# A hybrid decoder step on one core: one step boundary of the sample work removed on TensorE, two reductions moved on VectorE

## The reference

```
u = rms_norm(x);  proj = u @ w_in                        # 1024 -> 3592 columns
h_m = sigmoid(mo) * mlstm(mq, mk, mv, mi, mf, C, n, m)   # 4 heads of 64
h_r = retention(rope(rq), rope(rk), rv, S)               # 4 heads of 64
h_a = window_attention(aq, ak, av, k_buf, v_buf, ...)    # 8 heads, 2 kv heads, window 128
mix = concat(head_norm(h_m) * silu(mz), head_norm(h_r) * silu(rz), h_a * silu(az))
x   = x + mix @ w_out                                    # 1024 -> 1024
```

```
scores = einsum('bhtd,bhsd->bhts', qc, kc) * d_mat
o = einsum('bhts,bhse->bhte', scores, vc) + inter * einsum('bhtd,bhde->bhte', qc, S)
S_new = full * S + einsum('hs,bhsd,bhse->bhde', tail, kc, vc)
```

## Time and profile before

| what | value |
|---|---|
| runs of the kernel | 2145.33, 2147.58, 2148.93 us; median 2147.58 |
| the profiled execution, own time | 2145.33 us |
| its span, first to last instruction | 2143.5 us |
| PE busy | 2052.6 us (96%) |
| DVE busy | 1563.1 us (73%) |
| ACT busy | 881.6 us (41%) |
| POOL busy | 326.0 us (15%) |
| mean granted TensorE clock | 0.980 of full speed |
| output stage of layer 0 / layer 1, from their first matmuls | 872 / 1921 us |

### The profile page before, as it was taken

The page is one execution under the profiler, slowest core; times in us unless marked ns, Lnnn a source line. Parts: engine busy times, 40 slices in busy tenths (PEclk is TensorE's granted clock), DMA queues, the critical chain, the costliest instruction groups (busy, mean ns, idle before and its releaser), DMA issues.

```text
span 2143.5 us, 36369 instructions
## 1 busy us (share of the span) xinstructions
PE 2052.6 (96%) x12946; PEld 1159.4 (54%) x12946; DVE 1563.1 (73%) x3802; ACT 881.6 (41%) x2302; POOL 326.0 (15%) x352
## 2 busy tenths in 40 slices
PE   4799999999999999999988999999999999999997
PEld 2465555655555565444555555555565556554453
DVE  5777777777777777766365777777777777778866
ACT  5744444444444445331156444444444444461100
POOL 1111111111111111120010211111111111111200
PEclk9899999999999999999999999999999999999999
DMA  7411111111111114585541111111111111137642
GB/s 252 116 29 32 32 42 34 37 31 31 31 31 31 32 39 120 140 257 137 153 156 63 32 32 32 31 31 31 41 31 31 36 36 41 51 119 166 174 121 94
DMA packets 191788, 158.38 MB, mean 74 GB/s; under 512 B 151319, under 2 KB 165336, under 8 KB 191516
## 3 DMA queue, kind: packets, MB, share of 16 engines
q1 hardware_dynamic: 175684, 125.42, 21.7%
q0 software_dynamic: 7424, 29.43, 3.9%
q10 hardware_dynamic: 8568, 2.18, 0.5%
HBM read 85.35 MB, written 42.29 MB: 60 GB/s over the span
## 4 chain that ended last, share of the span: by engine, by line
PE 83%; DVE 12%; issue 2%; ACT 2%; DMA 1%; SPq 0%; DVEq 0%; ACTq 0%
PE J L544 51%; PE J L1257 12%; PE W L936 3%; PE W L956 3%; DVE W L537 2%; PE W L946 1%; PE W L1059 1%; PE W L1047 1%; PE W L1018 1%; PE J L993 1%; DVE ST L1805 1%; PE W L1038 1%; ACT junk L446 1%; DMA sc_xr<-in_x_sample 1%; PE W L922 1%
## 5 line engine op out<-in xcount | busy, mean ns | idle before, releaser
L544 PE MATMUL J<-W,x_mix 128*128 128x512 f16 (+2 forms) x3072 | 612.7, 357 | 5.9 <-ACT PB L1376 3.9
L544 PE MATMUL J<-W,uT_mix 128*128 128x512 f16 (+2 forms) x3072 | 613.5, 357 | 2.7 <-DVE W L537 2.6
L544 PEld LDWEIGHTS J<-W,x_mix 128*128 128x128 f16 x3072 | 300.0, 99 | 278.9 <-issue 14.9
L544 PEld LDWEIGHTS J<-W,uT_mix 128*128 128x128 f16 x3072 | 300.0, 99 | 276.3 <-issue 15.1
L1376 ACT ACTIVATE PB<-J,out_scale 128x512 f32<-128x512 f32 (+2 forms) x256 | 154.7, 604 | 357.6 <-PE J L544 348.9
L1257 PE MATMUL J<-W,EM_qkR_mix 128*128 128x512 f16 x480 | 115.6, 379 | 0.0
L1735 DVE TENSOR_TENSOR ge<-ge,gr 128x512 f32<-128x512 f32 (+1 forms) x96 | 57.4, 598 | 59.3 <-ACT gr L1313 59.3
L1346 ACT ACTIVATE ST<-ST,small 128x1024 f16<-128x1024 f32 x32 | 36.8, 1148 | 151.7 <-DVE small L1821 151.7
L1341 ACT ACTIVATE sc_xr<-sc_xr,small 128x128 f32<-128x128 f32 x256 | 98.6, 389 | 0.0
L1257 PE MATMUL J<-W,x_mix 128*128 128x512 f16 x400 | 97.9, 384 | 0.0
L1257 PE MATMUL J<-W,uT_mix 128*128 128x512 f16 x400 | 96.9, 381 | 0.0
(11 more groups left out here) (463 smaller groups left out, 3508.0 us busy)
## 6 DMA issues: line engine op xcount, KB each, us to landing
W<-in_w_in POOLq DMA_DIRECT2D x8, 2048.0 KB, 12.0
mix_d<-ST SPq DMA_DIRECT2D x32, 512.0 KB, 2.6
sc_xr<-in_x_prompt SPq DMA_DIRECT2D x20, 512.0 KB, 3.7
sc_xr<-x SPq DMA_DIRECT2D x20, 512.0 KB, 3.4
ST<-in_w_in POOLq DMA_DIRECT2D x4, 2048.0 KB, 12.9
W<-in_w_out SPq DMA_DIRECT2D x4, 2048.0 KB, 7.7
PB<-in_x_prompt SPq DMA_DIRECT2D x6, 512.0 KB, 3.7
x<-PB SPq DMA_DIRECT2D x6, 512.0 KB, 3.5
```

Of the source, the lines that this page charges most:

```text
L544: mm = nc.tensor.matmul(out, stationary(k, a), moving[:, k, b, :], start=(k == 0 and n == 0), stop=(k == KT - 1 and n == 2))
```

## The change

On PE the boundary between the sample's attention scores and the transposes of the rotated rows is removed: both are now in slot 9's step (before: slots 9 and 10). On DVE `inter(4)` and `inter(5)` leave slot 16's step, get a boundary of their own (`yield 13`) behind the mLSTM's state update, and so stand in slot 18's step. No arithmetic is changed.

```diff
@@ on_pe
                             kTS[64 * kv:64 * kv + 64, b, :], start=True, stop=True)
                 last_mm.then_inc(raised("scores_psum"), 1)
-                yield 5
-
                 pe.wait_ge(*seen("rope_done", layer))
                 for t in range(4):
                     last_mm = nc.tensor.transpose(T[1][:, 256 + t * TS:256 + (t + 1) * TS], PS[:, RQ + t * P:RQ + (t + 1) * P], idt)
@@ on_dve
                 V.tensor_tensor(sc, sc, bc(rden, WINDOW + DEC_SEQ), ALU.mult).then_inc(raised("pnorm"), 1)
-                inter(4)
-                inter(5)
                 yield 12
 
                 st(V.tensor_tensor(nu, nu, bc(tok[0:TS, 4:8], HD + 1), ALU.mult))
@@ on_dve
                 V.tensor_tensor(nst.rearrange("p k b -> p (k b)"), nst.rearrange("p k b -> p (k b)"),
                                 B[3][:, 260:276], ALU.add).then_inc(raised("state_m"), 1)
+                yield 13
+
+                inter(4)
+                inter(5)
                 yield 15
```

## The result

The changed kernel takes 2159.04 us (median of 5 runs, 2155.6 to 2160.3), the kernel before 2147.58 us (2145.33 to 2148.93). The ratio is 1.0054, 95% interval 1.0040 to 1.0069: slower by 11.5 us, where 9.6 were forecast. The profiled execution after has a span of 2155.5 us, 12.0 more than before. PE is busy 2058.6 us of it instead of 2052.6, with the same 12946 instructions.

The account below looks back on a forecast made before the run. PE, busy 96% of the span, was taken as the bound. Terms 2.5 + 1.5 + 0 + 4.1 + 1.5 = 9.6 us moved the median from 2147.58 to 2157.2 us, range 2152.5 to 2160.7.

Parts of the forecast that it names:

- Slot 9's wait: Layer 0: PE waits for POOL's rotation until about 937.8 instead of 935.31 for the maxima; slot 11 is 2.5 us late.
- The clock behind it: After PE stands about 4.9 us in layer 0's slot 9, the clock drops to 1.2 GHz and recovers; 1.5 us, bounds 0 and 3.0.
- Slot 10 in layer 1: Rotation long done and PE without idle; the same 0.39 us of transposes comes one slot earlier, costed at nothing.
- Layer 0's slot 19: PE's stall on the state update ends on the moved multiplies instead; scores start at 1001.8 against 1001.76, gain 0.
- The bounds of -5.8 and +3.5: Layer 0's slot 19: -5.8 if line 2808 isn't held, +3.5 if the hold stays where it is.
- Layer 1's slot 19: PE's products 6 and 7 wait 2.7 and 1.2 us for the moved multiplies: +4.1 us, plus 1.5 of lost clock.
- I give nothing back: Behind slot 20 both stages are paced by PE and loads follow the same chain, so the whole delay reaches the end.
- My list of signs: Expected waits, releasers and 0.5 clock would confirm; short line 2808, earlier rotation or a later stretch giving time back would refute.
- the free line 2808: Rival: in layer 0 DVE's line 2808 isn't held by POOL, slot 19 wins 5.8 us, 2151.4 us; chance 0.08.
- the emptier slot 16: Rival: both multiplies are done before PE enters slot 19's step in both layers; -1.8 us, 2145.8; chance 0.03.
- the rival without a loss in slot 9: Rival: the rotation is done in time, so PE doesn't wait in slot 9; 5.2 us slower, 2152.8; chance 0.05.
- a clock that holds: Rival: clock stays up after one or both stalls, 1.5 or 3.0 us less loss, 2154.2 to 2155.7 us; chance 0.20.

Follow-up runs that it names:

- run 1: Kernel before with only the PE half: boundary ahead of the transposes removed, the two reductions left in slot 16; 1.0013, +2.8 us.
- run 4: Changed kernel with POOL's sample rotation in layer 0 put ahead of its wait for the stored mix and the weight load; 1.0031 to the kernel before.
- run 3: Kernel before with the DVE half in layer 0 alone, reductions staying in slot 16 in layer 1; 1.0010, +2.1 us.
- run 5: Kernel before with the two DVE reductions in slot 18 and PE's products 6 and 7 moved to slot 20's step; 0.9987, -2.8 us.
- run 6: Kernel before with only PE's products 6 and 7 moved to slot 20's step, reductions left in slot 16; 1.0007, +1.5 us.
- run 8: Changed kernel with unread products ahead of PE's waits in layer 0's slot 9 and both layers' slot 19; 1.0032 to the kernel before, +6.9 us.
- run 2: Kernel before with only the DVE half: the two reductions in slot 18, PE boundary kept; 1.0031, +6.7 us.

## Why the prediction was right, point by point

The changed kernel's execution is compared at the same events of PE, so that only differences between neighbours count. It was already 0.65 us late at slot 9's scores (932.81 against 932.16), before anything of the change.

- **Slot 9's wait: forecast 2.5, measured 2.0** (4.41 us of idle where 2.46 was). The rotation came when it did before, while PE itself arrived 0.65 late. The mechanism was shown by runs 1 and 4.
- **The clock behind it: forecast 1.5 with bounds 0 and 3.0, measured 2.9.** From the start of the transposes to the end of slot 10 it is 8.7 us, where the same work takes 5.8 in the earlier trace rows. This term was mis-sized: I took the price of one low stretch behind a 3.1 us stall, and behind 4.4 us it was near twice that. Its starting point was also a draw: by the traces of runs 3, 5 and 6 the old stall in slot 9 costs 1.65 us in some executions, so the change adds less than 2.9 there on average. How much less isn't known. The two add to 4.8 us, which is PE's delay at slot 11's step: 952.19 - 946.70 - 0.65.
- **Slot 10 in layer 1: forecast 0.** PE shows no new idle there. Right.
- **Layer 0's slot 19: forecast 0, measured +1.2.** Slot 20 starts at 1010.81 instead of 1004.14, 6.7 late, against 5.5 at slot 11 (at slot 21, 7.0 late, so +1.5 with slot 20). Every event came as worked out: the 1.16 us gone, line 2808 held as before, the pair right behind the residual of slot 18. The term missed product 7: I priced it at 0.54 us by dividing the pair's 1.08 by two, which is a misreading of the earlier trace rows, since the two ran side by side. From its start to the transposes it is 2.32 us (1006.72 to 1009.04) where I had 1.16; 0.36 of the difference is the parting (run 8), 0.8 the clock. The bounds of -5.8 and +3.5 both stayed unused.
- **Layer 1's slot 19: forecast 4.1 + 1.5 = 5.6, measured 6.2.** Slot 20 starts 10.19 late (2060.62 against 2050.43), and PE had come into this stage's sample work 3.98 late (1989.83 against 1985.85 at the scores of slot 9). The waits are 2.55 and 0.70 us where I had 2.7 and 1.2; the second is shorter because product 6 alone takes 1.07 us and not 0.54. The clock is dearer, in slot 19's step and again in slot 20 (0.77 over 6.4 us, 1.5 us more by the end of that slot). By the end of slot 20 the loss is 7.7 us, 4.4 of waits and parting and 3.3 of clock. By the rule of the Trainium skill that the prediction weighed (TensorE: Matmul & The Clock Gate, "Why this matters for your kernels") the clock would have held here, since neither wait reaches the length that it names. The trace doesn't bear that out: 0.66 behind 2.55 and 0.70 us of idle, which stand one product apart.
- **"I give nothing back": wrong in detail, for the clock.** PE was 6.7 us late at slot 20 of layer 0, 7.0 at slot 22's step (1027.17 against 1020.21), 5.3 at the end of slot 24 (1048.76 against 1043.45) and 4.0 at slot 9 of layer 1. In layer 1 it was 10.2 late at slot 20, 11.7 at slot 22's step (2077.72 against 2066.06), 10.3 at slot 28 (2117.95 against 2107.63) and 12.0 at the end of the span. No queue made that up. PE did the same instructions between these points in less or more time, by the granted clock; the last 1.7 us are slot 28, 0.67 in the table above and 1.00 before. These are differences between two single executions, and nothing shows that the change causes them. My list of signs named a later stretch that gives time back as one against the forecast, and it did show.
- **Rivals.** The clock did not hold, line 2808 did not run free, slot 9 did wait, and the pair came late in layer 1. Each is excluded by the trace. By time run 3 excludes the free line 2808 and run 2 the emptier slot 16; run 1 leaves the rival without a loss in slot 9 only the edge of its interval (1.0004, against at most 1.0005), and run 8 speaks against a clock that holds.

The sum was 9.6 us, and 11.5 were measured. At the same events, to the end of slot 20 in each layer, waits and parting came to 6.8 us (2.0, 0.4, 4.4) where I had 6.6, and the added clock to 7.3 us (2.9, 1.1, 3.3) where I had 3.0. That the whole still came out close is in part luck: of these 14 us about 2.7 were made up in stretches that the change doesn't touch, and with the 0.65 from the start the profiled execution ends 12.0 us behind. The waits, their releasers and their places were right; the price of the clock was not. The 4.6 us of run 8 can't be set against my 3.0, since run 8 also lifts the clock behind layer 0's slot 19, where the kernel before pays too.

What stays open is the exact share of either half: they give 2.8 and 6.7 us, 2.1 less together than the whole, inside what the intervals allow.

## What to carry to other kernels

Moving work to a slot where its engine has time only helps if nobody who stands on the other side of a bank needs it sooner. List for each moved instruction the event it raises and who waits for that, and what is queued behind the waiter: here the moved multiplies free two banks, and PE's two products stood ahead of the work the move was to bring forward. A wait moved up by one boundary costs as much as the gap between the two arrivals, even if the work behind it is 0.4 us and fits into idle time. A stall of some microseconds on PE should be priced with the slower work behind it, here 2.7 to 3.3 us at each of the three places, and that price should be read from several executions: the same stall was free in one and cost 1.65 us in another. And before the time of a merged row is divided among its instructions, look whether they ran side by side: parted, each may take as long as both did.

## What the runs showed of the hardware that was not expected

Behind a stall the price of the lower clock moves about, between places and between executions. Behind 3.10 us, slot 19's scores to the end of slot 20 take 8.0 us in the kernel before (1001.76 to 1009.75) and 8.2 in run 1 (1006.25 to 1014.42), where full speed makes 6.4 (2049.17 to 2055.61), once with the slow part first and once with it last. Behind 4.41 us in slot 9 the loss was 2.9 us, near twice that, and behind 2.55 and 0.70 us in layer 1 it was 3.3. Slot 9's old stall of 2.3 to 2.5 us was free in the kernel before's trace and cost 1.65 us in runs 3, 5 and 6. The 1.6 us before slot 28, which no kernel here changes, were followed by a granted clock of 1.00 in two of the ten traces and by a lower one in eight.

The same work behind slot 22, with no wait in it, takes one of two times. From slot 22's step to the end of slot 24 the ten traces have it 20 times: 21.6 to 21.7 us 11 times and 22.9 to 23.3 us 9 times, both values in the same kernel (run 1: 21.72 in layer 0, 22.95 in layer 1). The step is a row of small products with 64 columns, and the granted clock falls part way through them, earlier or later. Runs of one kernel spread by some 6 us (the kernel before: 2142.9 to 2149.1 in 25 runs); such steps of 1.5 us are a part of it, and whether they are all of it was not tried. PE kept 2.4 GHz all through the filled waits of run 8 and behind them, with products whose results nobody reads.
